# Mixture-of-experts stage with 32 slots per request and expert, scatter summed in PSUM

## What is computed

```
g_idx  = argmax of 4 group logits              # per token
top_i  = top 2 of the 8 experts of that group
combine[token, expert] = group weight * normalised expert weight
hid = silu(h @ w_gate[e]) * (h @ w_up[e])      # 32 experts, 1024 -> 256
hid = hid * combine[..., e]
y   = sum over e of hid @ w_down[e]            # 256 -> 1024
```

## Time and profile before

| | |
|---|---|
| median of 3 runs | 1180.57 us (1175.22 to 1180.72) |
| profiled execution, span from first to last instruction | 1175.9 us (the page gives no other time of it) |
| PE busy | 1028.4 us, 87% |
| DVE busy | 388.2 us, 33% |
| ACT busy | 199.3 us, 17% |
| mean granted TensorE clock | 0.938 of full |
| HBM read | 329.38 MB, 282 GB/s over the span |

### The profile page before, as it was taken

One profiled execution on the slowest core, in us unless ns is written; L12 is line 12 of the kernel. 1 busy time (PEld: TensorE's weight loads), 2 busy tenths in 40 slices (PEclk: granted clock), 3 DMA queues, 4 the chain that ended last, 5 costly groups with the idle time before them and its releaser, 6 DMA issues.

```text
span 1175.9 us, 14167 instructions
## 1 busy us (share of the span) xinstructions
PE 1028.4 (87%) x5752; PEld 662.1 (56%) x5752; DVE 388.2 (33%) x724; ACT 199.3 (17%) x415; POOL 0.2 (0%) x4
## 2 busy tenths in 40 slices
PE   4499999999579999999929999999947999999993
PEld 1378757777454444444317876777846544444431
DVE  1212322222643333333281242221264323333326
ACT  0002113200022222211100131140002221111211
POOL 0000000000000000000000000000000000000000
PEclk7699999999779999999968999999975999999997
DMA  9566445578849999999734755436691799999960
GB/s 367 204 259 247 164 168 202 193 258 343 368 176 396 402 401 400 401 404 400 301 112 164 267 201 189 180 143 251 241 427 48 327 400 405 400 402 401 400 264 37
DMA packets 43198, 332.55 MB, mean 283 GB/s; under 512 B 5528, under 2 KB 7928, under 8 KB 13968
## 3 DMA queue, kind: packets, MB, share of 16 engines
q1 hardware_dynamic: 33552, 308.82, 65.4%
q10 hardware_dynamic: 9600, 23.07, 5.9%
HBM read 329.38 MB, written 2.49 MB: 282 GB/s over the span
## 4 chain that ended last, share of the span: by engine, by line
PE 84%; DVE 8%; DMA 4%; issue 2%; ACT 1%; ACTq 0%; DVEq 0%
PE ps L664 19%; PE ps L698 10%; PE ps L486 10%; PE ps L649 6%; PE ps L510 5%; PE ps L601 5%; PE ps L611 4%; PE ps L712 4%; PE ps L422 4%; PE ps L535 3%; PE ps L436 3%; PE ps L522 2%; PE ps L567 2%; PE ps L456 2%; PE ps L557 1%
## 5 line engine op out<-in xcount | busy, mean ns | idle before, releaser
L664 PE MATMUL ps<-expert_gate_up,gatheredT 128*64 128x512 f32 x1024 | 226.8, 595 | 2.2 <-DVE gatheredT L1277 2.2
L664 PEld LDWEIGHTS ps<-expert_gate_up,gatheredT 128*64 128x64 f32 x1024 | 71.6, 137 | 134.8 <-issue 133.8
L486 PE MATMUL ps<-hT,dense 128*128 128x256 f32 x512 | 114.2, 381 | 0.0
L698 PE MATMUL ps<-expert_down,hidT 128*64 128x512 f32 x512 | 113.7, 596 | 0.0
L486 PEld LDWEIGHTS ps<-hT,dense 128*128 128x128 f32 x512 | 96.1, 190 | 16.0 <-issue 3.6
L436 PE MATMUL ps<-const,h_tokens 128*128 128x128 f32 x64 | 14.4, 416 | 67.4 <-DVE h_tokens L1016 67.4
L698 PEld LDWEIGHTS ps<-expert_down,hidT 128*64 128x64 f32 x512 | 35.6, 136 | 66.2 <-issue 55.2
L649 PE MATMUL ps<-select,h_hi 128*128 128x256 f32 x256 | 69.5, 306 | 2.9 <-DVE select L1270 2.9
L422 PE MATMUL ps<-dense,cond 128*32 128x256 f32 x768 | 57.0, 420 | 16.6 <-ACT cond L797 9.4
L1304 DVE TENSOR_TENSOR y_lo<-ps,y_hi 128x512 fp32r<-128x512 f32 x64 | 44.3, 692 | 80.8 <-ACT y_hi L927 80.8
L649 PE MATMUL ps<-select,h_lo 128*128 128x256 f32 x256 | 66.4, 294 | 0.0
(11 more groups left out here) (197 smaller groups left out, 1118.2 us busy)
## 6 DMA issues: line engine op xcount, KB each, us to landing
expert_gate_up<-in_w_gu SPq DMA_DIRECT2D x64, 2048.0 KB, 12.0
expert_down<-in_w_dn SPq DMA_DIRECT2D x64, 1024.0 KB, 10.4
dense<-in_w_ada SPq DMA_DIRECT2D x48, 1024.0 KB, 4.8
dense<-in_w_in SPq DMA_DIRECT2D x28, 1024.0 KB, 6.2
dense<-in_w_o SPq DMA_DIRECT2D x8, 1024.0 KB, 6.3
dense<-in_w_out SPq DMA_DIRECT2D x8, 1024.0 KB, 7.2
shift<-ada_rows ACTq DMA_DIRECT2D x4, 1024.0 KB, 12.0
scale<-ada_rows ACTq DMA_DIRECT2D x4, 1024.0 KB, 7.9
```

The costliest lines, as they stand in the source:

```text
L486: last = mm(b[:, m * 256:(m + 1) * 256], w[:, k, m * P:(m + 1) * P], hT[:, k, :], start=(k == 0), stop=(k == KD - 1))
L664: last = mm(ps[64 * j:64 * j + 64, 4 + q, :], xgT[:, k, P * q + 64 * j:P * q + 64 * j + 64], w_gu[2 * q + j][:, k, :], start=(k == 0), sto ...
L698: last = mm(ps[64 * j:64 * j + 64, c, :], hidT[q][:, f, 64 * j:64 * j + 64], w_dn[2 * q + j][:, f, c * 512:(c + 1) * 512], start=(f == 0), ...
```

## The change

Each request gets 32 slots of its own per expert (`CAP = 32`). One iteration's four experts now have 4 x 32 slots of request 0 and 4 x 32 of request 1. The selection matrix is computed for all experts at the start in two instructions. The gather works on two iterations' slots at once (256 columns), each request apart, in every second iteration, after the hidden transposes; one bank holds one k. Gate/up and down run as matmuls of 32 columns, four side by side. The y tile of down is ordered by request, so that a request's scatter is one sum over 128 slots. The scatter of an iteration is issued in the next, a half behind each gate/up half, and sums over all eight iterations in banks 4 to 7; `y_acc` and its adds and memset are gone, and the gate multiplication reads PSUM. The combine weight is no longer in the hidden product but is the scale of y's copy and of `y_lo`. All four down loads now wait for all of down. The iterations on TensorE, ScalarE and VectorE are written out instead of looped; the counts of the experts are taken per request.

The diff, cut to its core. Of the removed lines those that the section before prints are left out; four levels of indentation are taken off.

```diff
-CAP = 64
+CAP = 32
 EPI = 4
 ITERS = NE // EPI
-MAX_ROUNDS = 2 * P // CAP
+MAX_ROUNDS = P // CAP
...
+        xgT = arena("gatheredT", 0, [P, KD, 2, 2 * EPI * CAP])
+        sel = arena("select", 16, [P, 2, NE * CAP], F32R)
+        selT = arena("selectT", 24, [P, 2, 2, P], F32R)
...
 def expert_load(l, g, i, first):
     m = M[l]
+    for q in range(2):
+        if not first:
+            sp.wait_ge(m["h_filled"], 2 * g + q - 1)
+        for j in (2 * q, 2 * q + 1):
+            src = io["w_gu"][l, ds(i * EPI + j, 1)].rearrange("o p k f -> (o p) k f")
+            sp.dma_start(w_gu[j][:, :, :], src).then_inc(m["gu_in"][j], 16)
+    if not first:
+        sp.wait_ge(m["y_filled"], 4 * g)
     for j in range(EPI):
-        if j % 2 == 0 and not first:
-            sp.wait_ge(m["h_filled"], g * 2 + j // 2 - 1)
-        src = io["w_gu"][l, ds(i * EPI + j, 1)].rearrange("o p k f -> (o p) k f")
-        sp.dma_start(w_gu[j][:, :, :], src).then_inc(m["gu_in"][j], 16)
-    for j in range(EPI):
-        if j % 2 == 0 and not first:
-            sp.wait_ge(m["y_filled"], g * 4 + j - 2)
         src = io["w_dn"][l, ds(i * EPI + j, 1)].rearrange("o p k f -> (o p) k f")
         sp.dma_start(w_dn[j][:, :, :], src).then_inc(m["dn_in"][j], 16)
-    mm(b[:, 0:NE], before, member[:, 0, :], start=True, stop=True)
-    mm(b[:, NE:2 * NE], before, member[:, 1, :], start=True, stop=False)
-    mm(b[:, NE:2 * NE], ones, member[:, 0, :], start=False, stop=True)
-    mm(b[:, 2 * NE:3 * NE], ones, member[:, 0, :], start=True, stop=False)
-    last = mm(b[:, 2 * NE:3 * NE], ones, member[:, 1, :], start=False, stop=True)
+    for s in range(2):
+        mm(b[:, s * NE:(s + 1) * NE], before, member[:, s, :], start=True, stop=True)
+    for s in range(2):
+        last = mm(b[:, (2 + s) * NE:(3 + s) * NE], ones, member[:, s, :], start=True, stop=True)
...
+    pe.wait_ge(ada_biased, ada_parts(l).stop)
+    def gather(n, pair):
+        cols = slice(pair * 2 * EPI * CAP, (pair + 1) * 2 * EPI * CAP)
+        for k in range(KD):
+            if k >= 2:
+                pe.wait_ge((m["xg_act"], m["xg_dve"])[k % 2], 4 * n + k // 2)
+            for s in range(2):
+                for hp, part in enumerate((h_hi, h_lo)):
+                    last = mm(ps[:, 2 + k % 2, s * 256:(s + 1) * 256], part[:, s, k * P:(k + 1) * P],
+                              sel[:, s, cols], start=(hp == 0), stop=(hp == 1))
+            last.then_inc(m["xg_filled"], 1)
+    def select_T(i):
+        for s in range(2):
+            picked = sel[:, s, i * P:(i + 1) * P].bitcast(F32)
+            tr(ps[:, 1, s * P:(s + 1) * P], picked, ident)
+            last = mm(ps[:, 1, 256 + s * EPI:256 + (s + 1) * EPI], picked, comb[:, s, i * EPI:(i + 1) * EPI],
+                      start=True, stop=True)
+        last.then_inc(m["selT_filled"], 1)
+    def gate_up(g, i, q):
+        for j in range(2):
+            pe.wait_ge(m["gu_in"][2 * q + j], g * 16 + 16)
+        for k in range(KD):
             for j in range(2):
                 for s in range(2):
...
+                    at_ = (i % 2 * EPI + 2 * q + j) * CAP
+                    r = 64 * j + 32 * s
+                    last = mm(ps[r:r + 32, q, :], xgT[:, k, s, at_:at_ + CAP],
+                              w_gu[2 * q + j][:, k, :], start=(k == 0), stop=(k == KD - 1),
+                              skip_group_check=True)
+        last.then_inc(m["h_filled"], 1)
+    def down(g, s):
+        for c in range(2):
+            if s:
+                pe.wait_ge(m["lo_done"], 4 * g + c + 1)
             for f in range(2):
...
+                for e in range(EPI):
+                    at_ = 64 * (e % 2) + 32 * s
+                    last = mm(ps[32 * e:32 * e + 32, 2 + c, :], hidT[:, e // 2, f, at_:at_ + CAP],
+                              w_dn[e][:, f, c * 512:(c + 1) * 512], start=(f == 0), stop=(f == 1),
+                              skip_group_check=True)
+            last.then_inc(m["y_filled"], 1)
+    def scatter(g, i, s, first):
+        for c in range(2):
+            pe.wait_ge(m["lo_done"], 4 * g + 2 * s + c + 1)
+            for hp, part in enumerate((y_hi, y_lo)):
+                last = mm(ps[:, 4 + 2 * s + c, :], selT[:, i % 2, s, :], part[:, s, c * 512:(c + 1) * 512],
+                          start=(first and hp == 0), stop=True, skip_group_check=True)
+        last.then_inc(m["sc_filled"], 1)
+    def moe_round(r, n0, g0):
+        pe.wait_ge(m["sel_ready"], 2 * r + 1)
+        gather(n0, 0)
+        pe.wait_ge(comb_ready, l + 1)
+        select_T(0)
+        for i in range(ITERS):
+            g = g0 + i
+            if i % 2 == 0:
+                pe.wait_ge(m["xg_act"], 4 * (n0 + i // 2) + 4)
+                pe.wait_ge(m["xg_dve"], 4 * (n0 + i // 2) + 4)
+            for q in range(2):
+                if q:
+                    pe.wait_ge(m["selT_copied"], g + 1)
+                gate_up(g, i, q)
+                if i:
+                    scatter(g - 1, i - 1, q, isinstance(r, int) and i == 1)
+            if i == 0:
+                pe.wait_ge(m["sel_ready"], 2 * r + 2)
+            pe.wait_ge(m["hid_done"], 2 * g + 2)
+            for q in range(2):
+                for f in range(2):
+                    last = tr(ps[:, 0, (2 * q + f) * P:(2 * q + f + 1) * P], hid[:, q, f * P:(f + 1) * P], ident)
             last.then_inc(m["hidT_filled"], 1)
...
+            if i + 1 < ITERS:
+                select_T(i + 1)
+            if i % 2 and i + 1 < ITERS:
+                gather(n0 + (i + 1) // 2, (i + 1) // 2)
+                pe.wait_ge(m["xg_act"], 4 * (n0 + (i + 1) // 2) + 4)
+                pe.wait_ge(m["xg_dve"], 4 * (n0 + (i + 1) // 2) + 4)
+            for j in range(EPI):
+                pe.wait_ge(m["dn_in"][j], g * 16 + 16)
+            pe.wait_ge(m["hidT_copied"], g + 1)
+            for s in range(2):
+                down(g, s)
+        for s in range(2):
+            scatter(g0 + ITERS - 1, ITERS - 1, s, False)
+    moe_round(0, 0, 0)
...
+    def gathered(n):
+        for k in range(0, KD, 2):
+            act.wait_ge(m["xg_filled"], 8 * n + k + 1)
+            actf(xgT[:, k, :, :], ps[:, 2, :].rearrange("p (s t) -> p s t", s=2),
+                 ACT.Copy).then_inc(m["xg_act"], 1)
+    def moe_round(n0, g0):
+        gathered(n0)
+        for i in range(ITERS):
+            g = g0 + i
+            for q in range(2):
+                act.wait_ge(m["h_filled"], 2 * g + q + 1)
+                actf(hid[:, q, :], ps[:, q, 0:FF], ACT.Silu).then_inc(m["silu_done"], 1)
+            act.wait_ge(m["hidT_filled"], g + 1)
+            actf(hidT[:, :, :, :], ps[:, 0, :].rearrange("p (q f t) -> p q f t", q=2, f=2),
                  ACT.Copy).then_inc(m["hidT_copied"], 1)
...
+            if i % 2 and i + 1 < ITERS:
+                gathered(n0 + (i + 1) // 2)
+            for s in range(2):
+                act.wait_ge(m["selT_copied"], g + 1)
+                for c in range(2):
+                    act.wait_ge(m["y_filled"], 4 * g + 2 * s + c + 1)
+                    if i or not isinstance(g0, int):
+                        act.wait_ge(m["sc_filled"], 2 * (g - 1) + s + 1)
+                    actf(y_hi[:, s, c * 512:(c + 1) * 512], ps[:, 2 + c, :], ACT.Copy,
+                         scale=wsl[:, i % 2, s:s + 1]).then_inc(m["hi_done"], 1)
+    moe_round(0, 0)
...
-    V.memset(y_acc[:, :, :], 0.0).then_inc(m["acc_done"], 4)
...
+    V.tensor_reduce(full[:, 0:1], b[:, 2 * NE:4 * NE], AX.X, ALU.max).then_inc(gone, 1)
...
+    def select(e0, e1):
+        shape = [P, 2, e1 - e0, CAP]
+        V.tensor_tensor(sel[:, :, e0 * CAP:e1 * CAP].rearrange("p s (e c) -> p s e c", c=CAP),
                         const[:, C_SLOT:C_SLOT + CAP].unsqueeze(1).unsqueeze(1).to_broadcast(shape),
...
+                        pos[:, :, e0:e1].unsqueeze(3).to_broadcast(shape),
                         ALU.is_equal).then_inc(m["sel_ready"], 1)
...
+    def gathered(n):
+        for k in range(1, KD, 2):
+            dve.wait_ge(m["xg_filled"], 8 * n + k + 1)
+            V.tensor_copy(xgT[:, k, :, :], ps[:, 3, :].rearrange("p (s t) -> p s t", s=2)
+                          ).then_inc(m["xg_dve"], 1)
+    def select_T(g, i):
+        dve.wait_ge(m["selT_filled"], g + 1)
+        for s in range(2):
+            V.tensor_tensor_reduce(wdiag[:, s, :], ps[:, 1, 256 + s * EPI:256 + (s + 1) * EPI],
+                                   const[:, C_DIAG:C_DIAG + EPI],
+                                   1.0, 0.0, ALU.mult, ALU.add, wsl[:, i % 2, s:s + 1])
+        V.tensor_copy(selT[:, i % 2, :, :], ps[:, 1, 0:2 * P].rearrange("p (s t) -> p s t", s=2)
+                      ).then_inc(m["selT_copied"], 1)
+    def moe_round(n0, g0):
+        gathered(n0)
+        select_T(g0, 0)
+        if isinstance(g0, int):
+            select(2 * EPI, NE)
+        for i in range(ITERS):
+            g = g0 + i
+            for q in range(2):
+                dve.wait_ge(m["silu_done"], 2 * g + q + 1)
```

(65 more changed lines are left out.)

158 lines of the change are left out of this document (19 added, 139 removed).

## The result

The changed kernel takes 1140.4 us, the median of four runs (1134.0 to 1141.5), against 1179.6 for the kernel before in the same comparison (1175.2 to 1180.7). The ratio is 0.966, with a 95% interval of 0.963 to 0.969. The medians give a gain of 39 us; the forecast was a gain of 46.0 and a time of 1134.6 us. In a second comparison it took 1136.8 (1134.6 to 1141.3, ratio 0.9635, 0.961 to 0.966), a gain of 43.7. So the forecast time lies at the lower edge of what the kernel does. The profiled execution took 1141.46 us with a span of 1139.3: 2.2 us lie around the span.

A forecast was written before the change was run, and what follows sets the result against it. TensorE paced the expert loops, with loads 1.9 us per iteration behind; loads then bind at 224.1 us a layer against 247.7. Less 0.6 for edges, two layers gain 46.0 off the 1180.57 median: 1134.6 us, range 1120 to 1157.

The forecast's parts named there:

- Gate/up and down: Expert loop on TensorE: four 32-column matmuls side by side keep a gate/up half at 7.02 us, at most 0.5 more.
- rival D: Expert loop: four tiles do not run side by side, gate/up and down take 42 us, total 1457 us; chance 0.04.
- Scatter halves: Scatter on TensorE: two halves of 1.02 us each per iteration instead of 4.42, one behind each gate/up half.
- The covered wait for the product: After gate/up: the scatter half covers the wait for silu and product, costed at nothing; 1.0 us without that cover.
- Gather: Gather on TensorE: 7.4 us per two iterations, 3.8 of it work, because two banks turn over and wait for copies.
- TensorE's layer: Sum of a layer's expert loop on TensorE alone: 217.3 us, iterations of 24.45 without and 31.65 with a gather.
- Loads: Expert weight loads of a layer: 224.1 us, with seven iterations at 29.4, above TensorE's 217.3, so DMA binds.
- Edges: Around the loops: first gather +1.1 us, after the last scatter -0.5, together +0.6 per layer.
- rival A: Expert loop loads cannot pass 403 GB/s on average; 10.3 us less per layer, 1160 us; chance 0.07.
- B: TensorE loses full clock in the gather; at 6 us per gather 1156 us, at 3 us about 1137; chance 0.15.
- C: Late down loads open holes in the load queue, 3 x 3 us per layer, 1153 us; chance 0.10.
- E: Unrolled code: instruction fetch stalls TensorE by 5 us per iteration, 1201 us; chance 0.02.

The follow-up runs named there:

- Run 1: Changed kernel, from iteration 1 on loading only half of each expert's gate/up weights, all instructions kept: 1118.4 us, ratio 0.9485.
- Run 7: Changed kernel with gate/up doing all k of one request, then all k of the other, same matmuls: 1277.75 us, ratio 1.083.
- run 3: Changed kernel with a gather in every iteration, four more per layer: 1171.1 us, ratio 0.993.
- run 6: Changed kernel with the first expert of iteration 1 loaded ahead into buffers that the dense stages leave free: 1132.1 us, ratio 0.960.
- runs 6 and 8: run 6, and run 6's kernel with the first expert of the next iteration loaded ahead in iterations 1 to 5 too: 1131.1 us, ratio 0.959.

## Why the prediction came out as it did

The mechanism was the one forecast: the loads take over from TensorE as the bound, and the loads' path is what a layer costs. Run 1 shows it: with fewer bytes and the same instructions the loops fall to 216.65. Step by step:

- **Gate/up and down** at 7.02 a half: 6.98. The upper bound of +0.5 was not needed, rival D is out. The small projection of the earlier trace rows was the right row to trust. Run 7 shows that most of D's price comes in another order: 12.2 a half instead of 14.0.
- **Scatter halves** 1.02: 1.05 to 1.13. The covered wait for the product: right. In iteration 0, without cover, the transposes wait 1.04, as costed.
- **Gather** at 7.4: 6.6 in the timeline, and 6.2 added in run 3 where 7.2 were costed. The turn of a bank was costed at 1.72, from a row in which gate/up, not the next matmul of a gather, waits for the copy (1.36). Here the last matmul of a bank is 1.0 to 1.1 ahead of what waits for its copy, and a turn took 1.4 to 1.5. An iteration with a gather is 30.8, not 31.65. It did not reach the time, since TensorE was not the bound.
- **TensorE's layer** at 217.3: 216.65 by run 1. Here two misses offset each other: three gathers that cost 0.9 less each, and a last iteration of 27.1 instead of 25.6. In that one I forgot the 0.8 of waiting for the transposed hidden values, which nothing covers in it, and took its down 0.1 and the tail 0.4 short.
- **Loads** at 224.1 a layer: 227.1 and 227.7. This is the term of the sum that was too small. Issue of the first load comes 0.3 behind the half. Seven iterations at 29.63 instead of 29.4 (430.40 to 548.91 is four of them) make 1.6. The rate of the window was right, 428, but not all that it counts are these weights: 12.58 MB in 29.63 us is 425. Behind the last down load come 9.53 us (568.50 to 578.03) instead of 9.0: down 7.13 for 7.0 and the tail 2.4 for 2.0, of which the weight in the two copies makes 0.15 (below). The remaining 0.6 to 1.1 lies before the landing of the last load and was not divided further.
- **Edges**: the first gather costs 0.55 and 0.84 more (0.97 and 0.93 in the second comparison's profile), forecast 1.1. The tail gains 0.75, forecast 0.5. VectorE's last multiplication starts 1.52 behind the end of the last scatter (578.03), where 2.25 was the time before and 1.75 was forecast (the counterpart of the last line of the earlier trace rows; its idle time counts from the last `y_lo`):

```profile
579.55 2.29 DVE L1343 TENSOR_TENSOR y_sum<-ps,gate 128x2048 f32<-128x2048 f32 x1 [2.31 <-issue]
```

So 3.0 to 3.6 us a layer, 6.6 in all, is the real error, all in the loads' path. The profiled span is 9.4 above the forecast one (1139.3 against 1129.9). The other 2.8 lie outside the loops, which lost 4.0 there (5.5 less the two gains of 0.75) where 1.2 was forecast. The second comparison's profile lost 0.1 there, so its 5.3 above the forecast is 6.4 in the loops less 1.1 outside. That the best times of the kernel meet 1134.6 owes something to luck: in both profiles the loops are over the forecast, in one of them the rest is under it. A slip in rival A changes nothing: 247.7 - 237.2 is 10.5, not 10.3.

**Rivals.** A (403 GB/s as the ceiling) is out: 428 over 206 us. The figure of 358 GB/s from the Trainium skill (DMA: Bandwidth & Descriptors, section Specifications) does not hold for this kernel, which runs on one core: the trace has 428 GB/s in the loops of both layers. B (the clock falls in the gather) is out by the window above: 5.89 of 7 us busy at clock 1.00, and the clock is 1.00 in all six gathers of the two loops. The rule that it leaned on (the Trainium skill, TensorE: Matmul & The Clock Gate, section A second HAM failure mode) does not show in this gather, though its banks turn over eight times. The clock did fall elsewhere, after some waits for weights (below). C does not appear in the kernel after; its hole does in run 6. E is out: TensorE's iterations without waits are within 1 us of the sum of their parts.

The thought that decided the case was the headroom: 1.9 us per iteration was all that the loads left under TensorE, while the change takes nearly 4 off it (31 over eight). A forecast from TensorE's layer alone, 217.3 instead of 224.1, would have been 1121 us.

## What to carry to other kernels

Before you price what a change takes off the bounding engine, find the rate of the next resource in a window where it has no hole, and turn it into a time per iteration; the gain ends there. A run that halves the bytes and leaves every instruction tells both sides: in the kernel before it changes nothing, in the kernel after it brings the 22 us that the loads keep. Once loads bound a loop, look at when buffers come free and in which order loads are issued: here loading ahead into the one queue brought 1 to 5 us of the 7.4 a loop by the profiles, and new holes and waits took much of the rest.

## What the runs showed of the hardware

**A wait of 2 us or more can cost clock, and need not.** A wait of 2.29 us for weights, behind some 200 us of nearly full work, was followed by a gate/up half of 8.77 us instead of 7.07. Windows ahead of it, around it and behind it (the clock is the third column from the end):

```profile
544.00:548.00 4.00, 2.62 (x28) 0.46 (x16) 1.94 (x3) 1.37 (x2) 0.00 (x0) 1.00 1.02 438
548.00:552.00 4.00, 3.09 (x18) 1.08 (x22) 0.16 (x1) 0.00 (x0) 0.00 (x0) 0.66 0.98 418
552.00:556.00 4.00, 4.00 (x40) 1.45 (x36) 0.00 (x0) 0.00 (x0) 0.00 (x0) 0.91 1.01 430
```

It came in both layers (2.18 us of wait in the other), twice more in the second comparison's profile (2.21 and 2.04) and again in runs 6 and 8 (2.17; 4.52 and 2.47). The length of the wait does not decide it: 2.11 us in layer 1 of this same trace, 2.23 in the second comparison's, and in run 6 even 2.61 left the next half at 7.07:

```profile
1080.08 7.07 PE L689 MATMUL ps<-expert_gate_up,gatheredT 128*32 128x512 f32 x64 [2.61 <-DMA expert_gate_up<-in_w_gu]
```

What decides stays open. The fall cost 1.7 us on TensorE, and no time of the loop here: down still waited 1.07 us for its weights behind it.

**A weight on a copy is not free.** The page's groups of the two evacuations of y, first after, then before:

```profile
L1318 DVE SCALAR_TENSOR_TENSOR y_lo<-ps,slot_weight,y_hi 128x512 fp32r<-128x512 f32 x64 | 48.0, 750 | 93.2 <-ACT y_hi L941 93.2
...
L941 ACT ACTIVATE y_hi<-ps,slot_weight 128x512 fp32r<-128x512 f32 x64 | 44.0, 687 | 91.2 <-PE ps L684 91.2
```

```profile
L1304 DVE TENSOR_TENSOR y_lo<-ps,y_hi 128x512 fp32r<-128x512 f32 x64 | 44.3, 692 | 80.8 <-ACT y_hi L927 80.8
...
L927 ACT ACTIVATE y_hi<-ps 128x512 fp32r<-128x512 f32 x64 | 38.2, 598 | 88.2 <-PE ps L698 88.2
```

The weight adds 58 ns on VectorE (750 against 692, with another instruction) and 89 ns on ScalarE (687 against 598). The two copies lie beside TensorE except in the last iteration of a layer, where one behind the other they make 0.15 of the 0.4 us by which the tail is longer than forecast.
